# Gate placement in a product-key expert kernel: the left operand written in fp32 by VectorE, without the bf16 one-hot and ScalarE's turned copy

## The reference, cut to what matters

```python
PEER_HEADS, PEER_NKEYS, PEER_TOPK, D_MODEL = 8, 128, 16, 1024      # 128*128 experts, 1024 + 128 tokens

def peer_retrieve(h, wq, keys):
    N = h.shape[0]
    q = (h @ wq).reshape(N, PEER_HEADS, 2, PEER_DHALF).astype(jnp.float32)
    s = jnp.einsum('nhpc,hpkc->nhpk', q, keys.astype(jnp.float32))
    sv, si = lax.top_k(s, PEER_TOPK)
    comb = sv[:, :, 0, :, None] + sv[:, :, 1, None, :]
    cv, ci = lax.top_k(comb.reshape(N, PEER_HEADS, PEER_TOPK * PEER_TOPK), PEER_TOPK)
    i1 = jnp.take_along_axis(si[:, :, 0], ci // PEER_TOPK, axis=-1)
    i2 = jnp.take_along_axis(si[:, :, 1], ci % PEER_TOPK, axis=-1)
    return i1 * PEER_NKEYS + i2, jax.nn.softmax(cv, axis=-1)

def peer_apply(h, expert, gate, u_tab, v_tab):        # by blocks of tokens
    ub, vb = jnp.take(u_tab, expert, axis=0), jnp.take(v_tab, expert, axis=0)
    a = jax.nn.gelu(jnp.einsum('nd,nhkd->nhk', h, ub), approximate=False)
    return jnp.einsum('nhk,nhkd->nd', gate * a, vb)
```

## Time and profile before

| | |
|---|---|
| median of three runs | 3460.2 us (3455.19 to 3461.52) |
| the profiled execution's own time | 3459.53 us |
| its span, first to last instruction | 3457.9 us |
| PE busy | 3047.9 us, 88% of the span |
| DVE busy | 2417.9 us, 70% |
| ACT busy | 935.4 us, 27% |
| POOL busy | 1461.4 us, 42% |
| granted TensorE clock, mean | 0.949 |

### The profile page before, as it was taken

One profiled execution on the slowest core, in us unless ns is written; L12 is line 12 of the kernel. 1 busy time (PEld: TensorE's weight loads), 2 busy tenths in 40 slices (PEclk: granted clock), 3 DMA queues, 4 the chain that ended last, 5 costly groups with the idle time before them and its releaser, 6 DMA issues.

```text
span 3457.9 us, 45275 instructions
## 1 busy us (share of the span) xinstructions
PE 3047.9 (88%) x16658; PEld 2337.0 (68%) x16658; DVE 2417.9 (70%) x4977; ACT 935.4 (27%) x1272; POOL 1461.4 (42%) x1188
## 2 busy tenths in 40 slices
PE   8899969243888837999999999999999999999996
PEld 1466634121555536888887888888888888999995
DVE  1233316998888886777776777776777777888888
ACT  0111112012888852222222212222222222222222
POOL 0000001765554526555545455554555554333335
PEclk9999989676999978999999999999999999999998
DMA  9611151974222238999999999998999998777765
GB/s 359 190 62 61 55 189 61 317 264 160 104 104 104 104 146 333 340 326 335 334 323 322 332 339 324 338 326 314 356 330 336 323 339 302 235 233 235 238 231 201
DMA packets 305763, 858.06 MB, mean 248 GB/s; under 512 B 25360, under 2 KB 108816, under 8 KB 303840
## 3 DMA queue, kind: packets, MB, share of 16 engines
q0 software_dynamic: 151344, 551.09, 44.5%
q1 hardware_dynamic: 154189, 305.27, 25.7%
q10 hardware_dynamic: 108, 0.22, 0.0%
HBM read 793.34 MB, written 63.15 MB: 248 GB/s over the span
## 4 chain that ended last, share of the span: by engine, by line
PE 58%; DVE 1%; DMA 1%; POOL 1%; issue 1%; ACT 0%; DVEq 0%; SPq 0%
PE y_ps L1771 25%; PE a_ps L1752 25%; PE picked_ps L1789 5%; PE uT_ps L1739 3%; DMA shared<-in_peer_u,ids 1%; POOL shared L1428 0%; POOL quad L1438 0%; DVE shared L1711 0%; DMA quad<-in_peer_v,idsT 0%; DVE shared L1591 0%; DVE shared L1699 0%; DVE quad L1617 0%; DVE quad L1699 0%; DVE quad L1711 0%; DVE v_lo L1582 0%
## 5 line engine op out<-in xcount | busy, mean ns | idle before, releaser
L1428 POOL DMA_INDIRECT shared<-in_peer_u,ids x384 | 446.0, 1162 | 639.5 <-DVE acts L1604 593.2
L1752 PE MATMUL a_ps<-h_hi,uT_lo 128*128 128x320 f32 x2048 | 644.1, 314 | 1.7 <-DVE h_lo L1687 1.7
L1752 PE MATMUL a_ps<-h_hi,uT_hi 128*128 128x320 f32 x2048 | 634.3, 310 | 0.0
L1752 PE MATMUL a_ps<-h_lo,uT_hi 128*128 128x320 f32 x2048 | 634.2, 310 | 0.0
L1591 DVE TENSOR_TENSOR shared<-shared,y_ps 128x512 f32<-128x512 f32 x640 | 436.4, 687 | 270.7 <-PE y_ps L1771 270.5
L1771 PE MATMUL y_ps<-v_hi,m_lo 128*128 128x512 f32 x1280 | 510.1, 398 | 14.1 <-DVE shared L1591 8.9
L1771 PE MATMUL y_ps<-v_lo,m_hi 128*128 128x512 f32 x1280 | 505.1, 395 | 0.0
L1771 PE MATMUL y_ps<-v_hi,m_hi 128*128 128x512 f32 x1280 | 502.3, 392 | 0.0
L1604 DVE CUSTOM_DVE_ANT_0 shared<-shared 128x1024 f32<-128x1024 f32 x384 | 464.8, 1220 | 20.4 <-DMA shared<-in_peer_u,ids 20.4
L1438 POOL DMA_INDIRECT quad<-in_peer_v,idsT x384 | 405.3, 1056 | 117.9 <-issue 117.9
L1752 PEld LDWEIGHTS a_ps<-h_hi,uT_lo 128*128 128x128 f32 x2048 | 385.9, 188 | 7.1 <-issue 2.1
(11 more groups left out here) (181 smaller groups left out, 4473.8 us busy)
## 6 DMA issues: line engine op xcount, KB each, us to landing
shared<-in_peer_u SPq DMA_DIRECT2D x128, 512.0 KB, 6.5
v_all<-in_peer_v SPq DMA_DIRECT2D x128, 512.0 KB, 6.4
gate_blocks<-dense SPq DMA_DIRECT2D x10, 4096.0 KB, 12.6
gates<-gate_blocks SPq DMA_DIRECT2D x64, 640.0 KB, 17.5
w_ada<-in_w_ada SPq DMA_DIRECT2D x12, 2048.0 KB, 10.9
x_in<-in_x_prompt SPq DMA_DIRECT2D x16, 512.0 KB, 4.5
shared<-in_w_in SPq DMA_DIRECT2D x8, 768.0 KB, 12.4
shared<-in_peer_wq SPq DMA_DIRECT2D x3, 2048.0 KB, 14.0
```

Of the source, the lines that this page charges most:

```text
L1428: pool.indirect_dma_start(out=rows[n % 4], out_offset=None, in_=u_table if n < DOTS else v_table, in_offset=bass.IndirectOffsetOnAxis(ap=i ...
L1752: last = nc.tensor.matmul(a_ps[n][:, 0:GROUP], lhs[s][:, k, :], rhs[:, k, tok], start=k == 0 and m == 0, stop=k == KD - 1 and m == 2)
```

## The change

`left_hot` and ACT's `left_rows` go. DVE compares the first keys, kept in fp32 and read with the token outside and the key inside, with an fp32 iota of 128 keys, and writes the result straight into the fp32 `left`. It waits for the PE product of batch b-2 where it waited for ACT's `left`. ACT's copy of the turned keys becomes two (fp32 for the left, bf16 for the right), POOL makes one iota more, and the counts of the semaphore `slotsT` go from two to three a tile; for the last tile a copy that nobody read is left out.

```diff
-        keyT = sbuf(nc, mem, "keyT", [P, 2, P], BF16)
+        leftT = sbuf(nc, mem, "leftT", [P, P])
+        rightT = sbuf(nc, mem, "rightT", [P, P], BF16)
-        left_hot = [sbuf(nc, mem, f"left_hot{s}", [P, NKEYS, BATCH], BF16) for s in range(2)]
+        iota_left = sbuf(nc, mem, "iota_left", [P, NKEYS])
...
             def take_slots(t):
-                nc.scalar.activation(keyT[:, :, :], x_ps[:, 0:2, :], ACT.Copy).then_inc(S.slotsT, 1)
+                nc.scalar.activation(leftT[:, :], x_ps[:, 0, :], ACT.Copy).then_inc(S.slotsT, 1)
+                nc.scalar.activation(rightT[:, :], x_ps[:, 1, :], ACT.Copy).then_inc(S.slotsT, 1)
                 nc.scalar.activation(gateT[:, :], x_ps[:, 2, :], ACT.Copy).then_inc(S.slotsT, 1)
             def take_index(t):
-                nc.scalar.activation(idsT[:, ORDER[t], :], x_ps[:, 0, :], ACT.Copy).then_inc(S.slotsT, 1)
+                act.sem_inc(S.slotsT, 1)
                 if ORDER[t] < MIXED:
+                    nc.scalar.activation(idsT[:, ORDER[t], :], x_ps[:, 0, :], ACT.Copy).then_inc(S.slotsT, 1)
                     nc.scalar.activation(gatesT[:, ORDER[t], :], x_ps[:, 2, :], ACT.Copy).then_inc(S.slotsT, 1)
                 else:
+                    act.sem_inc(S.slotsT, 1)
...
-            def left_rows(d, b):
-
-                act.wait_ge(S.left_hot, d * BATCHES + b + 1)
-                wait_for_placed(act, d, b)
-                nc.scalar.activation(left[b % 2][:, :, :], left_hot[b % 2][:, :, :].rearrange("p i t -> p t i"),
-                                     ACT.Copy).then_inc(S.left, 1)
...
             def hot_rows(d, b):
                 wait(dve, S.right, d * BATCHES + max(b - 1, 0))
-                nc.vector.tensor_tensor(right_hot[b % 2][:, :, :], key(1), keys_iota, ALU.is_equal)\
-                    .then_inc(S.right_hot, 1)
-                wait(dve, S.left, d * BATCHES + max(b - 1, 0))
-                nc.vector.tensor_tensor(left_hot[b % 2][:, :, :], key(0), keys_iota, ALU.is_equal)\
-                    .then_inc(S.left_hot, 1)
+                nc.vector.tensor_tensor(
+                    right_hot[b % 2][:, :, :],
+                    rightT[:, tokens].rearrange("p (o t) -> p o t", o=1).to_broadcast([P, NKEYS, BATCH]),
+                    iota_keys[:, :, :], ALU.is_equal).then_inc(S.right_hot, 1)
+                wait_for_placed(dve, d, b)
+                nc.vector.tensor_tensor(
+                    left[b % 2][:, :, :],
+                    leftT[:, tokens].rearrange("p (t o) -> p t o", o=1).to_broadcast([P, BATCH, NKEYS]),
+                    iota_left[:, :].rearrange("p (o i) -> p o i", o=1).to_broadcast([P, BATCH, NKEYS]),
+                    ALU.is_equal).then_inc(S.left, 1)
```

More of the change, by code:

```diff
@@ L702, in routing @@
     S = sems(nc, "route", "passed consts wq experts_in iota h2 keys_ps keysT q_ps q qT_ps qT scores "
-                               "scores_used shifted exp gate_ready keyed slotsT_ps slotsT left_hot left "
+                               "scores_used shifted exp gate_ready keyed slotsT_ps slotsT left "
                                "right_hot right place_ps placed out0 out1 best_key key_wide first_keyed dve expert picked row_in used "
@@ L826, in _ @@
                       allow_small_or_imprecise_dtypes=True).then_inc(S.iota, 1)
+            pool.iota(iota_left[:, :], pattern=[[1, NKEYS]], base=0, channel_multiplier=0,
+                      allow_small_or_imprecise_dtypes=True).then_inc(S.iota, 1)
             pool.iota(iota_keys[:, :, :], pattern=[[1, NKEYS], [0, BATCH]], base=0, channel_multiplier=0,
@@ L841, in place @@
                 d = t - FIRST_DENSE
-                pool.wait_ge(S.slotsT, t * 2 + 2)
+                pool.wait_ge(S.slotsT, t * 3 + 3)
                 for b in range(BATCHES):
@@ L931, in period @@
                 for b in range(BATCHES):
[L932 to L935, removed]
+                    if placed is not None and b:
+                        take_gates(placed - FIRST_DENSE, b - 1)
                     if prepare is not None and b in (4, 8):
@@ L957, in _ @@
             PER_TILE = 139
-            dve.wait_ge(S.iota, 2)
+            dve.wait_ge(S.iota, 3)
             dve.wait_ge(S.keysT, 1)
@@ L1104, in hot_rows @@
             def hot_rows(d, b):
[L1106 to L1110, removed]
+                tokens = slice(b * BATCH, (b + 1) * BATCH)
                 wait(dve, S.right, d * BATCHES + max(b - 1, 0))
-                nc.vector.tensor_tensor(right_hot[b % 2][:, :, :], key(1), keys_iota, ALU.is_equal)\
-                    .then_inc(S.right_hot, 1)
-                wait(dve, S.left, d * BATCHES + max(b - 1, 0))
-                nc.vector.tensor_tensor(left_hot[b % 2][:, :, :], key(0), keys_iota, ALU.is_equal)\
-                    .then_inc(S.left_hot, 1)
+                nc.vector.tensor_tensor(
[8 more added lines that the diff above has]
+                    ALU.is_equal).then_inc(S.left, 1)
             def period(choose, done, prepare):
@@ L1123, in rows @@
                     if b == 0 and done is not None:
-                        dve.wait_ge(S.slotsT, done * 2 + 2)
+                        dve.wait_ge(S.slotsT, done * 3 + 3)
                     if placed is not None:
@@ L1211, in period @@
                     if done is not None:
-                        pe.wait_ge(S.slotsT, done * 2 + 2)
+                        pe.wait_ge(S.slotsT, done * 3 + 3)
                     turn(prepare, 0)
```

## The result

The changed kernel takes 3501.8 us (median of 4 runs, 3498.4 to 3502.0), the kernel before 3459.5 in the same job: a ratio of 1.0122, 95% interval 1.0104 to 1.0139, so 42 us slower. The profiled execution of after took 3501.99, with a span of 3500.3 (before 3459.53 and 3457.9). The forecast was 3486, its range 3452 to 3499: the direction held, the size was 16 us short, and the result lies 3 us above the range.

The account below looks back on a forecast made before the run. Turns of DVE and POOL bound placement, ACT close behind; a period of 61.9 + 8.6 + 19.8 to 22.2 us, lower end taken: 5 x 5.3 = 26.5, less 0.3, on 3459.5, forecast 3486 us, range 3452 to 3499.

Parts of the forecast that it names:

- `left` in fp32 takes 1.14 us, all on the path: DVE in placement: the fp32 comparison takes 0.54 us more than bf16, adding 8.6 us a period, 43 in all.
- It takes turns with POOL in fp32 too: DVE and POOL in placement: fp32 with two SBUF operands blocks POOL like bf16, so all 0.54 us count.
- rival 1: DVE's fp32 comparison runs beside POOL: a period 8.4 us less, 42 us faster, 3418 us; chance 0.12.
- the two rules weighed in the prediction: GpSimd/VectorE blocking: only in two-port modes, or for any VectorE instruction with two SBUF inputs against a reading GpSimd.
- ACT's copy is worth 1.0 to 3.4 a period: ACT in placement: removing its turned copy of 170.2 us gains 1.0 to 3.4 us a period, 5 to 17 in all.
- The wait moved to DVE costs nothing: DVE ahead of `left`: waiting for PE's product of batch b-2 was taken to cost 0.
- the 2.4 us of slack: PE between placement products: time left for the query products before DVE's `left` needs the product of b-2.
- Rival 3: DVE waits for PE: each batch 0.7 us late adds 56 us, giving 3540 us; chance 0.03.
- The lower end, 5 x 5.3: Five placement periods: 26.5 us more in all, since nothing holds the last POOL instruction back from the next period.
- the forecast's 19.8 and 22.2: Placement period: us DVE stands still for uncovered POOL work; 19.8 if the last POOL instruction slips past the period's end.
- the sum's 90.3 to 92.7: Placement period after the change: 61.9 + 8.6 + 19.8 to 22.2 us, against 85.1 before.
- rival "no change": DVE in placement: declared waits of 35.0 us go as 43.2 of work comes; about 3463 us; chance 0.09.

Follow-up runs that it names:

- e1: Changed kernel, but POOL fills `right` with zeros and reads nothing: 3394.4 us, ratio to the kernel before 0.9802.
- e4: Changed kernel, but DVE's comparison for `left` covers 64 of 128 keys, the other half staying zero: 3456.5 us, ratio to the kernel before 0.998.
- e2: Kernel before, but POOL fills `right` with zeros and reads nothing: 3454.1 us, ratio to the kernel before 0.9974.
- e8: Kernel before, same instructions reordered: DVE's rows under searches where possible, turned slots and copies first on PE and ACT: 3461.5 us, ratio 0.9998.
- e9: Changed kernel, same instructions reordered: DVE's rows under searches where possible, turned slots and copies first on PE and ACT: 3462.1 us, ratio to before 1.0000.
- e7: Changed kernel with three buffers of `left`, so DVE waits for the product of batch b-3: 3488.5 us, ratio to the kernel before 1.0075.
- e3: Changed kernel, but DVE fills `left` with zeros instead of comparing: 3460.6 us, ratio to the kernel before 0.9995.
- e6: Changed kernel with `right` and `left` both made by DVE in eight instructions each, no POOL in the placement: 3526.2 us, ratio to before 1.0186.
- e5: Changed kernel with POOL's turning and gate multiplication given to ACT as eight scaled copies a batch: 3563.8 us, ratio to the kernel before 1.0296.

## Why the prediction was right in direction and short in size

- *`left` in fp32 takes 1.14 us, all on the path*: right. It lasts 1.216, and the next instruction starts 1.13 us after it (948.90 and 950.03).
- *It takes turns with POOL in fp32 too* (against rival 1): right, though what stands still for POOL is not what I named (`right_hot`) alone, but four instructions of `chosen_ranks` above all. POOL takes 3.25 beside it, and without POOL's read a period falls by 20.9 us (e1). Of the two rules weighed in the prediction the one of the Trainium skill's page SBUF — State Buffer, section "Who interferes with whom", is borne out: two SBUF inputs contend with a reading GpSimd, and here they do so in fp32 as in bf16. That page of the Trainium skill also lists copies, casts and `tensor_scalar` among what can take the shared pair; the 2.81 us of `digits` and the 2.48 of the cast agree.
- *ACT's copy is worth 1.0 to 3.4 a period*: right in the order of this kernel (1.9 in e4; e2's 2.2 is another quantity, the period without the turns and with ACT). In the order of e8 and e9 the same relief is worth all that the longer comparison costs.
- *The wait moved to DVE costs nothing*: **this step failed.** It costs 12.7 us of standing (15 waits, the longest 1.0), and 12.2 us of the periods by e7. I took the slack from batches that follow one another at POOL's pace. At batches 2 and 10 POOL is kept out by a run of DVE's instructions, most with two operands, PE stands 4 to 5 us for it, and then its product takes 3.8 us at the lower clock: the 2.4 us of slack are gone. Rival 3 named this wait, and the lower clock as a reason, with every batch late and a price of 56 us; three batches a period were late, for a quarter of that.
- *The lower end, 5 x 5.3, since the last POOL instruction slips past the period*: wrong as a reason. That instruction (1008.23, 3.18 us) still holds L1066, which takes 2.97 instead of 1.22, because DVE's wait for the widened keys fell from 2.0 to 0.3. In numbers the two nearly cancel. DVE's own list is 61.9 + 8.7 - 1.7 = 68.9; the wait is 2.5; so 92.5 - 71.4 = 21.1 are turns, between the forecast's 19.8 and 22.2. That 92.5 lies inside the sum's 90.3 to 92.7 is luck: the moved wait is not in that sum.
- *The size*: 92.5 against 90.3 a period is 5 x 2.2 = 11 us, about what e7 gives back. The other 5 of the 16 stand behind the stage, and their cause stays open.
- *The rival "no change"* fell: DVE's declared waits went from 44.9 to 36.3 us, but POOL's work stayed as long as it was and held up other instructions of DVE.

Open: which engine goes first where both are ready. After `right_hot` and `left` POOL gets in ahead of L1028, L1045, L1048 and L1055 here, but at 947.19 it stays out through several instructions of DVE; and in e3 it got through beside a fill when searches followed, but not when a short two-operand instruction did. No run here sets the order alone.

## What to carry to other kernels

Taking work off an engine that is second in line is worth only the distance to the first, and what is paid for it is paid in full where the first engine is: read both limits before you trade. When two engines take turns, count the work that has to be covered and look for what covers it, instruction by instruction; shortening or freeing one victim moves the wait to the next. And judge a change together with the order of the work: here it cost 1.2% in one order, nothing in another, and was part of a version 0.55% faster than before in a third, in which the kernel before was not run.

## What the hardware showed that I had not expected

- A fill of 128x1024 fp32 on DVE takes 0.91 us, and POOL beside it 2.40 or 3.3 to 3.4, by what DVE does next (e3).
- `tensor_scalar` on 128x128 fp32 with scalars from a column costs 0.196 us with one and 0.256 with two, by the distance of starts (1.57 and 2.05 for eight in e6); the mean duration in the lines is 275 and 335 ns.
- A scaled ACT copy of 128 elements with a strided bf16 source comes every 0.425 us (e5).
